# Forgetting attention in a two-layer trunk: q and k projected with the weights on the stationary side

## The reference

```python
proj = h @ w_in                                  # (256, 2048) @ (2048, 3*2048 + 16)
q, k, v, f_logit = jnp.split(proj, [D, 2 * D, 3 * D], axis=-1)   # 16 heads of 128
cum = cumsum(log_sigmoid(f_logit + b_f))         # per head, over the tokens
s = einsum('bqhd,bkhd->bhqk', q, k) * Dh ** -0.5 + cum[q] - cum[k]
p = softmax(where(causal, s, -inf));  o = p @ v;  y = o @ w_o
```

## Time and profile before

| what | value |
|---|---|
| median of 3 runs | 2277.46 us |
| the profiled execution | 2275.42 us |
| its span (first to last instruction) | 2273.5 us |
| busy share of PE, DVE, ACT | 95%, 69%, 44% |
| mean granted clock of TensorE, of 2.4 GHz | 0.990 |

### The profile page before, as it was taken

One profiled execution on the slowest core, in us unless ns is written; L12 is line 12 of the kernel. 1 busy time (PEld: TensorE's weight loads), 2 busy tenths in 40 slices (PEclk: granted clock), 3 DMA queues, 4 the chain that ended last, 5 costly groups with the idle time before them and its releaser, 6 DMA issues.

```text
span 2273.5 us, 24980 instructions
## 1 busy us (share of the span) xinstructions
PE 2166.5 (95%) x9786; PEld 1771.3 (78%) x9786; DVE 1568.7 (69%) x1774; ACT 997.0 (44%) x1313; POOL 104.9 (5%) x207
## 2 busy tenths in 40 slices
PE   4789989999999999999999999999999999999997
PEld 2377767888888888888788888878888888888885
DVE  5789879877677877778876555678775555454556
ACT  1056635444343344443544555554444433444433
POOL 2111100000000000000000000000000000000000
PEclk9999999999999999999999999999999999999998
DMA  9998996778888888888667666957886656655563
GB/s 389 419 369 321 367 345 219 274 292 298 270 317 324 322 323 297 295 320 327 220 224 270 225 228 223 287 167 251 295 283 166 230 191 194 195 186 193 195 221 121
DMA packets 146021, 605.47 MB, mean 266 GB/s; under 512 B 23920, under 2 KB 24176, under 8 KB 119408
## 3 DMA queue, kind: packets, MB, share of 16 engines
q1 hardware_dynamic: 109424, 398.31, 50.0%
q0 software_dynamic: 27648, 201.34, 24.1%
q10 hardware_dynamic: 8832, 4.23, 0.7%
HBM read 601.68 MB, written 2.13 MB: 266 GB/s over the span
## 4 chain that ended last, share of the span: by engine, by line
PE 81%; DVE 9%; DMA 8%; ACT 1%; issue 1%; POOL 0%; ACTq 0%; DVEq 0%; POOLq 0%
PE ps L1417 51%; PE ps L1423 25%; DMA ada_head<-in_ada_w 5%; DVE wlo L859 2%; DMA gate_rows<-mod 2%; DVE ada_w L883 1%; PE ps L1433 1%; PE ps L1404 1%; DMA raw<-in_mla_w_o 1%; PE ps L1593 1%; DVE ada_head L883 1%; DVE ada_low L883 0%; DVE gate L883 0%; ACT whi L506 0%; DMA ada_w<-in_ada_w 0%
## 5 line engine op out<-in xcount | busy, mean ns | idle before, releaser
L859 DVE TENSOR_TENSOR wlo<-raw,whi 128x1024 fp32r<-128x1024 f32 (+2 forms) x721 | 873.8, 1217 | 608.6 <-ACT whi L506 607.8
L506 ACT ACTIVATE whi<-raw 128x1024 fp32r<-128x1024 f32 (+2 forms) x721 | 759.2, 1055 | 1098.0 <-PE ps L1423 982.7
L1417 PE MATMUL ps<-whi,hT_hi 128*128 128x512 f32 x1880 | 588.3, 394 | 2.3 <-DVE hT_lo L1187 2.3
L1417 PE MATMUL ps<-whi,hT_lo 128*128 128x512 f32 x1880 | 580.5, 390 | 0.0
L1423 PE MATMUL ps<-wlo,hT_hi 128*128 128x512 f32 x1880 | 502.9, 389 | 0.0
L1417 PEld LDWEIGHTS ps<-whi,hT_lo 128*128 128x128 f32 x1880 | 353.5, 188 | 74.3
L1423 PEld LDWEIGHTS ps<-wlo,hT_hi 128*128 128x128 f32 x1880 | 353.0, 188 | 74.0
L1417 PEld LDWEIGHTS ps<-whi,hT_hi 128*128 128x128 f32 x1880 | 349.3, 188 | 72.3 <-DVE hT_lo L1187 2.7
L883 DVE CUSTOM_DVE_ANT_0 ada_w<-ada_w,c_bc,cols 128x2048 f32<-128x2048 f32 x144 | 337.7, 2346 | 14.6 <-DMA ada_w<-in_ada_w 14.5
L1417 PE MATMUL ps<-whi,uT_hi 128*128 128x512 f32 x672 | 207.2, 390 | 0.0
L1417 PE MATMUL ps<-whi,uT_lo 128*128 128x512 f32 x672 | 207.0, 389 | 0.0
(11 more groups left out here) (232 smaller groups left out, 1469.2 us busy)
## 6 DMA issues: line engine op xcount, KB each, us to landing
raw<-in_ffn_w SPq DMA_DIRECT2D x528, 512.0 KB, 4.4
ada_w<-in_ada_w POOLq DMA_DIRECT2D x144, 1024.0 KB, 5.8
raw<-in_fox_w_in SPq DMA_DIRECT2D x96, 512.0 KB, 4.3
ada_head<-in_ada_w POOLq DMA_DIRECT2D x17, 1024.0 KB, 21.7
raw<-in_mla_w_o SPq DMA_DIRECT2D x32, 512.0 KB, 8.2
raw<-in_fox_w_o SPq DMA_DIRECT2D x32, 512.0 KB, 4.5
gate<-in_ada_w POOLq DMA_DIRECT2D x13, 1024.0 KB, 10.1
ada_low<-in_ada_w POOLq DMA_DIRECT2D x10, 1024.0 KB, 10.4
```

What stands on the lines that cost most here:

```text
L506: nc.scalar.activation(whi[:, s, 0:n], raw[:, s, 0:n], ACT.Copy).then_inc(hi_ready, 1)
L859: nc.vector.tensor_tensor(wlo[:, s, 0:n], raw[:, s, 0:n], whi[:, s, 0:n].bitcast(F32), ALU.subtract).then_inc(lo_ready, 1)
L1417: nc.tensor.matmul(ps[:, 2 * pair + t, 0:width], a[:, t * P:(t + 1) * P], w_hi, start=(first and c == 0 and a is hi), stop=False)
```

## The change

q and k of FoX (not v, not MLA) are projected with 128x128 of weights as the stationary side and the tokens streaming, so that each head's result comes out with its features on the partitions, as the scores need it. The transposes and copies of FoX's q and k leave. ACT's wait before overwriting q and k becomes `scored`. The two buffers keep their size and place; only what lies where in them is new.

```diff
@@ proj_done (ACT)
-                        act.wait_ge(qk_turned if b < 2 else pv_done, H + (g - 1) * HG)
+                        act.wait_ge(scored if b < 2 else pv_done, H + (g - 1) * HG)
@@ attention (ACT): the copy to qkT
-                    if i < H:
+                    if i < H and rotary:
                         act.wait_ge(qk_turned, g + 1)
@@ PE, new
+            def turned_unit(pair, parts, first, end):
+                s = pl.unit % RING
+                def products(w, moving, start, stop):
+                    for h in range(HG):
+                        ins = nc.tensor.matmul(ps[:, 2 * pair + h // 2, h % 2 * S:(h % 2 + 1) * S],
+                                               w[:, h * DH:(h + 1) * DH], moving,
+                                               start=start and h % 2 == 0, stop=stop and h % 2 == 1)
+                    return ins
+                pe.wait_ge(hi_ready, pl.unit + 1)
+                for c, (hi, lo) in enumerate(parts):
+                    for a in (hi, lo):
+                        products(whi[:, s, c * NB:(c + 1) * NB], a, first and c == 0 and a is hi, False)
+                pe.wait_ge(lo_ready, pl.unit + 1)
+                for c, (hi, lo) in enumerate(parts):
+                    ins = products(wlo[:, s, c * NB:(c + 1) * NB], hi, False, end and c == UC - 1)
+                ins.then_inc(units_used, 1)
+                pl.unit += 1
+            def turned_part(slot, pair, t, parts, low, first, end):
+                for c, (hi, lo) in enumerate(parts):
+                    w = (wlo if low else whi)[:, slot, c * NB:(c + 1) * NB]
+                    for a in ((hi,) if low else (hi, lo)):
+                        for h in range(HG):
+                            o = h % 2 * S + t * P
+                            ins = nc.tensor.matmul(ps[:, 2 * pair + h // 2, o:o + P],
+                                                   w[:, h * DH:(h + 1) * DH], a[:, t * P:(t + 1) * P],
+                                                   start=(first and c == 0 and a is hi and o == 0),
+                                                   stop=(end and c == UC - 1 and h % 2 == 1))
+                return ins
...
@@ norm_turn(1) takes turned_part for its first 4 units, product(..., turned=True) for the next 4
+                first_part = turned_part if k == 1 else part
...
@@ projection
-                    product(r % PAIRS, KC, hT_hi, hT_lo)
+                    product(r % PAIRS, KC, hT_hi, hT_lo, turned=r < 2 * PAIRS)
@@ attention (PE): no transposes where not rotary; the scores read q and k where they were copied to
+                    if i == 0:
+                        pe.wait_ge(turned_out, pl.turn)
+                    if i < H and rotary:
...
+                        if rotary:
+                            pe.wait_ge(qk_copied, m + 1)
                             pe.wait_ge(qp_copied, m // 2 + 1)
+                            q, k = qkT[:, m % 2, 0:S], qkT[:, m % 2, S:2 * S]
+                        else:
+                            evicted(i - 1, blocks - 1)
+                            q, k = q_tile(i - 1), k_tile(i - 1)
...
+            def head(tile):
+                return lambda h: tile[:, (h // HG) % 2, h % HG // 2, h % 2 * S:(h % 2 + 1) * S]
+            attention(1, head(fox_q), None, head(fox_k), local(fox_v))
```

More of the change, by code:

```diff
@@ L1458, in pair_free, with product @@
                     pe.wait_ge(pair_read[block % 2], pair_uses(block, block % 2))
-            def product(j, chunks, hi, lo, width=NB):
+            def product(j, chunks, hi, lo, width=NB, turned=False):
                 if j == 0:
                     pair_free(pl.block)
-                unit(pl.block % 2, width,
-                     [(hi[:, UC * j + c, :], lo[:, UC * j + c, :]) for c in range(UC)],
-                     j == 0, UC * (j + 1) == chunks)
+                parts = [(hi[:, UC * j + c, :], lo[:, UC * j + c, :]) for c in range(UC)]
+                if turned:
+                    turned_unit(pl.block % 2, parts, j == 0, UC * (j + 1) == chunks)
+                else:
+                    unit(pl.block % 2, width, parts, j == 0, UC * (j + 1) == chunks)
                 if UC * (j + 1) == chunks:
@@ L1497, in norm_turn @@
                     pe.wait_ge(hi_ready, pl.unit + m + 1)
-                    part((pl.unit + m) % RING, pair, 0, chunks[m], False, m == 0, False)
+                    first_part((pl.unit + m) % RING, pair, 0, chunks[m], False, m == 0, False)
                 pe.wait_ge(norm_dve, T * k + 2)
@@ L1502, in norm_turn @@
                     pe.wait_ge(lo_ready, pl.unit + m + 1)
-                    part((pl.unit + m) % RING, pair, 0, chunks[m], True, False, False)
+                    first_part((pl.unit + m) % RING, pair, 0, chunks[m], True, False, False)
                 pe.wait_ge(norm_act, 4 * k + 3)
@@ L1508, in norm_turn @@
                     slot = (pl.unit + m) % RING
-                    part(slot, pair, 1, chunks[m], False, m == 0, False)
-                    part(slot, pair, 1, chunks[m], True, False, False).then_inc(units_used, 1)
+                    first_part(slot, pair, 1, chunks[m], False, m == 0, False)
+                    first_part(slot, pair, 1, chunks[m], True, False, False).then_inc(units_used, 1)
                     if m == 0:
@@ L1516, in norm_turn @@
                     pe.wait_ge(turned_out, first + m + 1)
-                    product(m, KC, hT_hi, hT_lo)
+                    product(m, KC, hT_hi, hT_lo, turned=k == 1)
             def projection(layer, k):
@@ L1563, in attention @@
                             pe.wait_ge(qk_copied, g)
-                        else:
-                            pe.wait_ge(turned_out, pl.turn)
                         for n, tile in enumerate((q_tile, k_tile)):
@@ L1581, in attention @@
                         m = g - 1
-                        pe.wait_ge(qk_copied, m + 1)
                         if rotary:
+                            pe.wait_ge(qk_copied, m + 1)
                             pe.wait_ge(qp_copied, m // 2 + 1)
+                            q, k = qkT[:, m % 2, 0:S], qkT[:, m % 2, S:2 * S]
+                        else:
+                            evicted(i - 1, blocks - 1)
+                            q, k = q_tile(i - 1), k_tile(i - 1)
                         if i >= 2:
@@ L1591, in attention @@
                             o = ps[:, 5, a:a + n]
-                            q = slice(t * P, (t + 1) * P)
-                            ins = nc.tensor.matmul(o, qkT[:, m % 2, q], qkT[:, m % 2, S:S + n],
+                            tokens = slice(t * P, (t + 1) * P)
+                            ins = nc.tensor.matmul(o, q[:, tokens], k[:, 0:n],
                                                    start=rotary, stop=not rotary and t == T - 1)
                             if rotary:
-                                ins = nc.tensor.matmul(o, qpT[:, m // 2 % 2, q], kpT[:, m % 2, 0:n],
+                                ins = nc.tensor.matmul(o, qpT[:, m // 2 % 2, tokens], kpT[:, m % 2, 0:n],
                                                        start=False, stop=True)
@@ L1766, in _ @@
                     pl.turn += 1
-            attention(1, local(fox_q), None, local(fox_k), local(fox_v))
+            def head(tile):
+                return lambda h: tile[:, (h // HG) % 2, h % HG // 2, h % 2 * S:(h % 2 + 1) * S]
+            attention(1, head(fox_q), None, head(fox_k), local(fox_v))
             w_o(1)
```

1 line of the change is left out of this document (removed).

## The result

The changed kernel took 2288.32 us (median of 9 runs, 2284.71 to 2306.37), the kernel before 2276.25 us (9 runs, 2272.57 to 2278.63). The ratio is 1.0067, 95% interval 1.0048 to 1.0086: slower. The forecast was 2286.4 us, in a range of 2274 to 2300. Two of the nine runs lie outside that range, at 2303.2 and 2306.4 us, with a mean granted clock of 0.979 and 0.980 where the others have 0.986 to 0.991. The profiled execution took 2285.93 us.

A forecast was written before the change was run, and what follows sets the result against it. PE was taken to bound the kernel, one for one. Whole units +9.6, split start +6.4 and transposes -7.1 gave +8.9 us, a median of 2286.4 us, in a range of 2274 to 2300 us.

The forecast's parts named there:

- PE's pitch sets the price: In q and k projection, a load and 256-column matmul pair costs 0.120 us, columns at 2.4 GHz plus 0.0133.
- The ceiling of 0.123: Upper bound on the 256-column pair if load time 0.110 and overhead 0.0133 us add up; whole units then cost +13.9 us.
- the loads that show: Rival for 256-column pairs: loads partly exposed, 0.130 us or more, +26 us; fully, 2397 us; chance 0.11, in full 0.02.
- the nearest row of before: Forget-logit unit, 256 columns behind 16-column loads, 0.1173 us a pair; as rival +5.0 us, chance 0.18.
- 60 whole units: Whole q and k units outside the split start: 2.88 us each instead of 2.72, +9.6 us, all on the path.
- The split start: In norm_turn(1), four units cut to 128 tokens run at the loads' pitch, 0.112 us; +6.4 us over three steps.
- The transposes: Removing four per head over 16 heads of FoX, 0.45 us for four, saves 7.1 us, all on the path.
- ACT's copies, and the waits on `scored` and `evicted`: In FoX's ticks, dropping ACT's 16 copies and changing the waits of ACT and PE costs or gains 0 us.
- The sum: Whole kernel: +9.6 + 6.4 - 7.1 = +8.9 us, median 2286.4 us (+0.39%).
- The chances by outcome: Whole kernel's time against before: faster 0.09, same 0.19, slower 0.72.
- the pitch at which nothing changes: 256-column pair time below which the kernel becomes faster than before, put at about 0.1135 us.
- The clock: Rival: granted clock falls in norm_turn(1)'s split start, 1.5 us per 3.4 us stretch, 3 for two; 2289 us; chance 0.04.

The follow-up runs named there:

- same_side_256: Kernel before, with its 60 whole q and k units streaming 256 weight columns per matmul instead of 512, activations still stationary; 2285.94 us, ratio 1.0040.
- no_turn: Changed kernel with all q and k units projected as before but still without FoX's transposes and copies (scores not the reference's); 2269.37 us, ratio 0.9969.
- v_first: Changed kernel with the first head group projected in the order v, q, k, so norm_turn(1) streams 512 columns; 2281.35 us, ratio 1.0016.
- after_again: Changed kernel run again with no edit; 7 runs, median 2303.61 us (2283.77 to 2309.04), ratio 1.0095.
- late_256: Changed kernel whose norm_turn(1) waits for both token tiles, then does the first 4 units whole, streaming 256 tokens; 2286.75 us, ratio 1.0036.
- split_only: Kernel before with only norm_turn(1)'s first 4 units streaming 128 tokens, weights stationary; 7 runs at 2279.5 to 2284.5 us, 5 at 2300.8 to 2307.2, ratio 1.0057.
- twin: Changed kernel with v first in the first group and each high-weight load serving the tokens' high and low parts in 512 columns; 2271.72 us, ratio 0.9984.
- narrow_all: Changed kernel with every turned q and k unit streaming 128 tokens twice instead of 256 once; 2472.39 and 2478.86 us, ratio 1.0868.
- the second profile: Profiled execution of the unedited changed kernel's repeat, one of its four runs at 2303.6 to 2309.0 us.

## Why the prediction was right, and what it missed

1. *PE's pitch sets the price.* Right. 0.120 us per 256-column pair was forecast from two other widths and measured to the nanosecond. The ceiling of 0.123 and the loads that show weren't needed; the nearest row of before, 0.1173 behind small loads, would have misled, and in this trace that unit itself shows 0.1134.
2. *60 whole units.* Forecast +9.6, measured 60 x 0.145 = +8.7; the term is off by the mean unit before, 2.735 and not 2.72 us.
3. *The split start.* Forecast +6.4, measured +6.1 at the full clock. Each step came within 0.2 us of where it was put: the transposes 7.17 us after the first matmul (forecast 7.2), DVE's last split behind them, 3.10 us per unit of the second token tile (3.14).
4. *The transposes.* Forecast -7.1, measured -7.14.
5. *ACT's copies, and the waits on `scored` and `evicted`.* Zero, as forecast: PE has no gap anywhere in B, in this kernel as in the one before. (56 x 0.145 - 7.14 = +0.98 is the growth of B itself, from which the 0.145 was taken, and shows nothing more; the 0.143 of `same_side_256`, which has none of these new waits, agrees.)
6. *The sum.* +8.9 forecast; the sections give 8.7 + 6.1 - 7.1 = +7.7 us at the full clock. The ten runs of sixteen at a clock of 0.986 or more have a median of 2286.3 us, 10 over before. The 2 us between I can't place; they may lie ahead of section A, whose start scatters by 8 us over the profiles (1112.7 to 1120.9), but that is not shown. The chances by outcome in the prediction (0.09, 0.19, 0.72) are not quite what its own cases add up to (0.08, 0.16, 0.76), and by its own terms the pitch at which nothing changes is 0.1138, not 0.1135.
7. *The clock: right place, wrong size.* I gave this rival 0.04 and +1.5 to +3 us, since I took a low stretch to end after 3.4 us as in the earlier trace rows and counted two at most. It came in 6 of 16 runs and costs 20.6 us, as the low clock stays for the whole stage. What was wrong in this rival is the length of the stretch: in the earlier trace rows it ended within a 512-column stream, and here no such stream came. A stretch of 3.4 us in a wide start, on the other hand, costs nothing (A is 31.80 in `no_turn` and 31.82 in `v_first`), because waits follow that take it up; the split start has no such waits left. The long stretch is also the larger part of why the ratio is 1.0067 and not the 1.004 of my sum: without the two low runs of the nine the mean of the rest gives 1.0050. The advice of the Trainium skill, same page, section "Why this matters for your kernels", to keep TensorE continuously busy for the full clock, would not have helped: PE was busy for all of the 44.4 us.

That the median of nine lies inside the range owes something to luck. Two of those nine had the long low stretch; in `after_again` four of seven did, and their median, 2303.61, lies outside it. What is right without luck is the mechanism of the sum and its size at the full clock.

What makes the clock fall in one run and not in the next is open. The same pauses of PE (0.26 or 0.27, then 1.47 or 1.48 us) stand at the start of the stage in every profile but that of `late_256`. The clock then fell in kernels with and without the change (`no_turn`, `v_first`, `split_only`, `twin`, `narrow_all`, the second profile) and not in the others, the first profile of the same changed kernel among them. That what follows decides how long it lasts is shown, by `split_only` against `v_first` and `late_256`.

## What to carry to other kernels

Count load and matmul pairs, not only columns: a different operand order that does the same multiplications in twice as many pairs costs the fixed part of each once more, here 0.145 us a unit by measurement (12 x 0.0133 = 0.16 by the pitch), and that ate more than the 64 transposes were worth. Before giving up on the order, look for a way to widen the moving side again, as `twin` did. And be wary of a stream of 128-column pairs right behind a pause of PE: the time of one run may show nothing, so look at the clock of several.

## What the runs showed of the hardware that was not expected

- At 2.4 GHz an fp32r pair costs its columns plus 0.0133 us for 512, 384 and 256 columns; at 1.2 GHz there is nothing on top (512 columns in 0.43 us; four pairs of 256 in 0.85 us in `late_256`).
- Pairs with 128 columns go at the pace of the loads, 0.111 us at the full clock and 0.213 at the low one (32 in 6.86 us in the second profile): loads slow down with the clock as streams do (one shows as 0.333 us in place of 0.192).
- The low clock outlasted 44.4 us (the second profile and `split_only`) and 85.3 us (`narrow_all`) of PE without a gap, in 128-column pairs and a few transposes, up to the last 2 to 4 us; the same pairs ran at the full clock in the ticks.
- A low stretch of 3.4 us cost nothing in the profiles where PE had a wait for ACT to come (`no_turn`, `v_first`, `twin`), and 0.7 us where it fell just behind that wait (section C of the changed kernel).
